# Block 2 of a two-block network: another order of TensorE's work inside a channel block

## The chip, the cores and the metric

The kernel runs on one core of one Trainium2 chip. The metric is the device time of one execution in microseconds; smaller is better. The kernel before has a median of 3219.48 us over 3 runs, from 3214.33 to 3221.94 us. Of the engines this text speaks of PE (TensorE, the matrix engine), DVE (VectorE), ACT (ScalarE), POOL (GpSimd) and SP (the queue that issues the weights' DMAs).

## What is computed

The network takes 1024 tokens of 1024 channels. A first block (two layers of convolution and sparse attention) is followed by a second one, and the change is in the second. There, eight projections of the normalised input are made (`xa`, `ga`, `q`, `f`, `v`, `g`, `m_a`, `m_b`), and two recurrences run over the tokens:

```python
proj = h @ w_in
xa, ga, q, f, v, g, m_a, m_b = jnp.split(proj, SPLIT_POINTS, axis=-1)
xa = causal_depthwise_conv(xa, conv_w, conv_b)
y_a = rg_lru(xa, w_r, b_r, w_i, b_i, lam) * jax.nn.gelu(ga)
...
log_f = jnp.log(jnp.maximum(f_gate, F_MIN))
kf = (1.0 - lb) * jax.nn.sigmoid(-zf)
o = rms_norm(hgrn2_chunkwise(qf, kf, log_f, vf), hg_norm)
y_b = o.reshape(B_, S_, HG_HEADS * HG_DV).astype(h.dtype) * jax.nn.silu(g)
y = jax.nn.sigmoid(m_a) * y_a + jax.nn.sigmoid(m_b) * y_b
return y @ w_out
```

`rg_lru` needs two more products of the convolved `xa`, in blocks of 256 channels: `r` and `i`. `hgrn2_chunkwise` is, for each head of 128 channels, causal linear attention in which the weight of key s for query t is the product of the forget gates between them.

## The kernel before

**Tiling.** The second block works through four channel blocks `b` of 256 channels, that is, two HGRN heads `c` each. A wide product is the sum of three bf16 matmuls (`mm3`, lines 275 to 277: high part by high, low by high, high by low), and its result for 128 channels and all 1024 tokens goes to one of two PSUM tiles of the pool `big`. `gemm_f` makes one such result in two halves of 512 tokens, with a call `between` them. Its eight k-steps are 24 matmuls a half; for `r` and `i` there are only two k-steps, so 6 matmuls a half.

**The order of a channel block on PE** is written out by hand: `xa`, `f`, `q` (two results each), the four tiles `tp` of `v` (token-major, 48 matmuls of 256 columns a tile), and then twelve `units`: r0, i0, r1, i1, ga0, ga1, ma0, ma1, gg0, gg1, mb0, mb1.

**The HGRN steps.** The decayed attention of one head is built by doubling. `hsteps` lists twelve steps for each head: `diag` (line 1004: the products on the diagonal, 8 matmuls of 128 columns in f32), the levels 0 to 6 (line 1052: 8 matmuls of 64 columns in f32), then `tr` (a transposition), `ds`, `o` and `ss`. Between two levels DVE must act: it copies the products under a mask into `PTT` (line 2105), folds the forget gates (line 2112) and scales the half of the queries `QE` and of the keys `KF` that the next level reads (lines 2113 and 2114). After `diag` it copies (line 2083) and multiplies `QE` by the gates (line 2086). So a level on PE waits for DVE, and DVE for the level before. In the kernel before, unit `u` takes the steps `2u` (between the halves of its product) and `2u + 1` (behind it); that puts `diag` and the levels 0 to 6 of head 0 into r0, i0, r1 and i1.

**Other work around it.** ACT evacuates each product in the same order (`evac`, line 1413; the tiles of `v`, line 1443). DVE's queue goes through the convolution, the gates `FG`, the keys `KF` (lines 2066 to 2068), the low part of `xa` (line 2071), and then through the steps in order. POOL splits each weight chunk of 1 MB into its bf16 parts (lines 550 and 557) for a ring of four chunks; it starts a split when PE has finished with the chunk four places earlier (`chunk_used`) and the DMA has landed. The order of chunks is xa, f, q, v, ri, ga, ma, gg, mb, so the end of `v` on PE releases the split of `gg`, and the end of i1 that of `mb`.

Of the kernel before, what the change touches and what calls it, by code (L numbers as in the profile page):

```python
# [23 lines left out]
P = 128  # L24
# [71 lines left out]
def build(nc, ap, events):  # L96

    ctx = ExitStack()
    with ctx:
# [88 lines left out]
        def mark(sem, *what, by=1):  # L188

            counts[sem.name] = counts.get(sem.name, 0) + by  # L190
            assert (sem.name, *what) not in seen, (sem.name, what)
            seen[(sem.name, *what)] = counts[sem.name]
            return by
# [5 lines left out]
        def when(sem, *what):  # L199

            return events[(sem.name, *what)] if events else 1
# [49 lines left out]
        def take(pe, pool, *what):  # L251

            n = turns.get(pool, 0) % len(pools[pool])
            turns[pool] = turns.get(pool, 0) + 1
            out, ids = pools[pool][n]
            if events:
                for before in dict.fromkeys(last_use[i] for i in ids if i in last_use):
                    for sem, value in events[("read", *before)]:
                        pe.wait_ge(sems[sem], value)
            for i in ids:  # L260
                last_use[i] = what
            slot[what] = n
            return out
# [8 lines left out]
        def mm3(pe, out, a, b, start, stop):  # L272

            (ah, al), (bh, bl) = a, b
            pe.matmul(out, ah, bh, start=start, stop=False)  # L275
            pe.matmul(out, ah, bl, start=False, stop=False)  # L276
            return pe.matmul(out, al, bh, start=False, stop=stop)  # L277

        def chunk(l, name, kt):
            n = CHUNK_AT[(l, name)] % RING  # L280
            return [w[:, n, :].rearrange("p (k c) -> p k c", k=kt) for w in (w_hi, w_lo)]
# [124 lines left out]
        units = [("r", 0), ("i", 0), ("r", 1), ("i", 1)] + [(c, n) for c in ("ga", "ma", "gg", "mb") for n in range(2)]  # L406
        FINISH = (10, 11)
        hsteps = [(c, st) for c in range(2) for st in ["diag"] + list(range(7)) + ["tr", "ds", "o", "ss"]]


        ADA_PIECES = [(0, n, kp) for n in range(4) for kp in range(KT // 2)]
# [150 lines left out]
        def _(pe):  # L562
            def gemm_f(l, name, ct, key, rhs=hT, kts=KT, cols=None, pool="big", cw=256, N=T, between=None):

                w = chunk(l, name, CH // cw)
                g = take(pe, pool, *key)
                c0 = ct * P if cols is None else cols[0]
                m = P if cols is None else cols[1] - cols[0]
                for half in range(N // 512):
                    for k in range(kts):  # L570
                        ins = mm3(pe, g[0:m, half * 512:(half + 1) * 512], [x[:, k, c0:c0 + m] for x in w],
                                  [x[:, k, half * 512:(half + 1) * 512] for x in rhs], k == 0, k == kts - 1)
                    if half == 0 and between:
                        between()
                ins.then_inc(s_gemm, mark(s_gemm, *key))

            def chunk_used(l, name, sem):

                seen[("used", CHUNK_AT[(l, name)])] = (sem.name, counts[sem.name])
# [394 lines left out]
            for b in range(4):  # L974
                if b == 0:
                    first_gemm(2, "xa0", [("xa", 0, 0), ("xa", 0, 1)])
                for c in ("xa", "f", "q") if b else ("f", "q"):
# [1 line left out]
                    gemm_f(2, f"{c}{b}", 0, (c, b, 0))  # L979
                    gemm_f(2, f"{c}{b}", 1, (c, b, 1))  # L980
                    chunk_used(2, f"{c}{b}", s_gemm)
                pe.wait_ge(s_w_split, when(s_w_split, CHUNK_AT[(2, f"v{b}")]))
                w = chunk(2, f"v{b}", KT)
                for tp in range(4):
                    g = take(pe, "big", "v", b, tp)
                    for j in range(2):
                        t0 = (2 * tp + j) * P
                        for k in range(KT):
                            ins = mm3(pe, g[:, j * 512:j * 512 + 256], [x[:, k, t0:t0 + P] for x in hT],
                                      [x[:, k, :] for x in w], k == 0, k == KT - 1)  # L990
                    ins.then_inc(s_gemm, mark(s_gemm, "v", b, tp))
                chunk_used(2, f"v{b}", s_gemm)

                def hgrn(c, st):
                    key = (b, c, st)
                    v = VT[:, :, c * P:(c + 1) * P]
# [45 lines left out]
                    else:  # L1042
# [9 lines left out]
                            ins = pe.matmul(g[:, s * 64:(s + 1) * 64].rearrange("p (j h) -> p j h", h=h), KF[c][:, s * P:(s + 1) * P], q, start=True, stop=True)  # L1052
                        ins.then_inc(s_hgrn, mark(s_hgrn, *key))

                for u, (c, n) in enumerate(units):
                    if c in "ri":
                        if u == 0:
                            pe.wait_ge(s_w_split, when(s_w_split, CHUNK_AT[(2, f"ri{b}")]))
                            pe.wait_ge(s_rg_dve, when(s_rg_dve, "xs_lo", b, 1))
                        gemm_f(2, f"ri{b}", None, (c, b, n), rhs=XS, kts=2, cols=((c == "i") * 256 + n * P, (c == "i") * 256 + (n + 1) * P), cw=512,  # L1060
                               between=lambda: hgrn(*hsteps[2 * u]))
                        if u == 3:
                            chunk_used(2, f"ri{b}", s_gemm)
                    else:
                        pe.wait_ge(s_w_split, when(s_w_split, CHUNK_AT[(2, f"{c}{b}")]))
                        gemm_f(2, f"{c}{b}", n, (c, b, n), between=lambda: hgrn(*hsteps[2 * u]))
                        if n == 1:
                            chunk_used(2, f"{c}{b}", s_gemm)
                    hgrn(*hsteps[2 * u + 1])

            def first_two(part, g):
                pe.wait_ge(s_hgrn_dve, when(s_hgrn_dve, "y2_lo", 2, 1))
# [47 lines left out]
        def _(act):  # L1120
# [298 lines left out]
            for b in range(4):  # L1419
# [49 lines left out]
                            freed(s_hgrn_act, "hs", *key, half)  # L1469

                for u, (c, n) in enumerate(units):
                    hgrn(*hsteps[2 * u])
                    if c == "r":
                        act.wait_ge(s_rg_dve, when(s_rg_dve, "xc", b, 1))
                        evac(R_[n], ACT.Sigmoid, "r", b, n, bias=v_("b_r", 2 * b + n))
                    elif c == "i":
                        if b:
                            act.wait_ge(s_rg_dve, when(s_rg_dve, "ya2", b - 1, 1))
                        evac(IT[n], ACT.Sigmoid, "i", b, n, bias=v_("b_i", 2 * b + n))
                        if n == 1:  # L1480
                            act.wait_ge(s_dve_setup, when(s_dve_setup, "sp8"))
                            for m in range(2):
                                act.wait_ge(s_read_act, when(s_read_act, "r", b, m))
                                act.activation(TH[m], R_[m], ACT.Tanh, scale=SP8[:, 2 * b + m:2 * b + m + 1]).then_inc(s_rg_act, mark(s_rg_act, "th", b, m))
                            for m in range(2):
                                act.wait_ge(s_rg_act, when(s_rg_act, "th", b, m))
                                act.activation(R_[m], R_[m], ACT.Exp, scale=NSP8[:, 2 * b + m:2 * b + m + 1]).then_inc(s_rg_act, mark(s_rg_act, "a", b, m))
                    elif c == "ga":
                        if n == 0:
                            for m in range(2):  # L1490
                                act.wait_ge(s_rg_dve, when(s_rg_dve, "one_a2", b, m))
                                act.activation(XC[m], XC[m], ACT.Sqrt).then_inc(s_rg_act, mark(s_rg_act, "mult", b, m))
                        act.wait_ge(s_rg_dve, when(s_rg_dve, "one_a2", b, n))
                        evac(TH[n], ACT.Gelu_apprx_tanh, "ga", b, n)
                    elif c == "ma":
                        act.wait_ge(s_rg_dve, when(s_rg_dve, "ha", b, n))
                        evac(IT[n], ACT.Sigmoid, "ma", b, n)
                    elif c == "gg":
                        act.wait_ge(s_hgrn_dve, when(s_hgrn_dve, "lvl", b, n, 0))
                        evac(FG[n], ACT.Silu, "gg", b, n)  # L1500
                    else:
                        act.wait_ge(s_hgrn, when(s_hgrn, b, n, "tr", 1))
                        evac(KF[n], ACT.Sigmoid, "mb", b, n)
                    hgrn(*hsteps[2 * u + 1])
                    for m in range(2):
                        if u == FINISH[m]:
                            act.wait_ge(s_hgrn_dve, when(s_hgrn_dve, "y2_f", b, m))
                            act.activation(Y2[0][:, 2 * b + m, :], OO, ACT.Copy).then_inc(s_hgrn_act, mark(s_hgrn_act, "y2_hi", b, m))
# [65 lines left out]
        def _(dve):  # L1574
# [473 lines left out]
            for b in range(4):  # L2048
# [71 lines left out]
                def TOT(i):  # L2120

                    at = 1024 - (1024 >> (i - 1))
                    return TB[:, at:at + (1024 >> i)]

                for u, (c, n) in enumerate(units):
                    if (c, n) == ("gg", 0):
                        for m in range(2):
# [5 lines left out]
                        if b < 3:  # L2133

                            dve.wait_ge(s_rg_dve, when(s_rg_dve, "ya2", b, 1))
                            dve.memset(XAP[:, :, 0:3], 0.0).then_inc(s_dve_setup, mark(s_dve_setup, "pad2", b + 1))
                    hgrn(*hsteps[2 * u])
                    hgrn(*hsteps[2 * u + 1])
                    if (c, n) == ("i", 1):
                        for m in range(2):  # L2140
                            dve.wait_ge(s_read_act, when(s_read_act, "i", b, m))
# [250 lines left out]
```

## Time and profile before

| | |
|---|---|
| median of 3 runs | 3219.48 us (3214.33 to 3221.94) |
| profiled execution, span from first to last instruction | 3213.2 us |
| PE busy | 3009.0 us (94%) |
| DVE busy | 1870.8 us (58%) |
| ACT, POOL busy | 1109.3 us (35%), 1033.7 us (32%) |
| granted TensorE clock, mean | 0.966 of 2.4 GHz |
| the four channel blocks of block 2 | about 1512 to 2470 us of the span |

The profile gives one execution. Its span leaves out what lies before the first and behind the last instruction; its own whole time isn't shown, so the median is used beside it, 6.3 us above the span. Starts are in us from the start of the span. In the chain of waits a piece lasts until its successor could go on, and "x16" there is 8 matmuls with their 8 weight loads.

### The profile page before, as it was taken

The numbers are of one execution on the slowest core, as the hardware profiler recorded it, in microseconds if no ns is written. First come the engines' busy times: TensorE is split into PE (matmuls) and PEld (weight loads), VectorE is DVE, ScalarE is ACT, GpSimd is POOL, SyncE is SP. The second block draws the span as 40 slices with busy tenths as digits, with TensorE's granted clock in tenths as the row PEclk, the third lists the DMA queues.
The fourth block names the chain that finished last, engine by engine and source line by source line (L and its number), as shares of the span: only waits on it lengthen the run. The fifth ranks groups of instructions, "written<-read, shape, count | busy, mean of one in ns | idle before, by whom it ended". The sixth has DMA issues, their size and how long they took to land.

```text
span 3213.2 us, 48564 instructions
## 1 busy us (share of the span) xinstructions
PE 3009.0 (94%) x19842; PEld 1864.1 (58%) x19842; DVE 1870.8 (58%) x3077; ACT 1109.3 (35%) x1972; POOL 1033.7 (32%) x1000
## 2 busy tenths in 40 slices
PE   7979987999979978989999999999999989999998
PEld 7439865884439657864555555555565434444443
DVE  2575796773589986644365365365365374545455
ACT  2353545662366635643222222232122221111112
POOL 2301365000512570002512412422322235555552
PEclk9988998999989989999999989999989999999999
DMA  7423232002201330022111101101102101111111
GB/s 243 138 59 106 82 120 86 15 22 99 89 14 43 120 129 28 14 83 77 66 40 40 53 27 40 53 27 40 53 27 92 41 27 53 53 53 53 53 53 73
DMA packets 49165, 207.13 MB, mean 64 GB/s; under 512 B 4488, under 2 KB 9776, under 8 KB 32304
## 3 DMA queue, kind: packets, MB, share of 16 engines
q1 hardware_dynamic: 42288, 195.63, 17.7%
q10 hardware_dynamic: 6656, 8.39, 0.8%
q8 instruction: 158, 2.59, 0.3%
q14 instruction: 63, 0.52, 0.1%
HBM read 187.22 MB, written 16.79 MB: 63 GB/s over the span
## 4 chain that ended last, share of the span: by engine, by line
PE 78%; DVE 16%; ACT 3%; issue 3%; POOL 1%; DMA 0%; SPq 0%; DVEq 0%; ACTq 0%; POOLq 0%
PE big L275 16%; PE big L276 16%; PE big L277 16%; PE banks L275 6%; PE banks L277 5%; PE banks L276 5%; PE banks L1052 4%; DVE arena L1771 2%; PE banks L911 2%; DVE arena L1996 1%; PE big L587 1%; PE banks L587 1%; DVE arena L2160 1%; DVE arena L1976 1%; PE banks L590 1%
## 5 line engine op out<-in xcount | busy, mean ns | idle before, releaser
L557 POOL TENSOR_TENSOR w_lo<-stage,w_hi 128x512 bf16<-128x512 f32 x464 | 594.7, 1315 | 398.2 <-ACT w_hi L1239 397.5
L550 POOL CAST w_hi<-stage 128x512 bf16<-128x512 f32 x376 | 248.6, 704 | 1427.3 <-PE big L277 1232.3
L275 PE MATMUL big<-ht_hi,w_hi 128*128 128x512 bf16 x1184 | 448.7, 379 | 11.7 <-DVE arena L2023 6.5
L277 PE MATMUL big<-ht_hi,w_lo 128*128 128x512 bf16 x1184 | 448.7, 379 | 0.0
L276 PE MATMUL big<-ht_lo,w_hi 128*128 128x512 bf16 x1184 | 448.7, 379 | 0.0
L275 PE MATMUL big<-w_hi,ht_hi 128*128 128x256 bf16 (+1 forms) x1280 | 384.6, 300 | 20.8 <-POOL w_lo L557 9.1
L276 PE MATMUL big<-w_lo,ht_hi 128*128 128x256 bf16 (+1 forms) x1280 | 384.1, 300 | 0.0
L277 PE MATMUL big<-w_hi,ht_lo 128*128 128x256 bf16 (+1 forms) x1280 | 383.4, 300 | 0.0
L1784 DVE TENSOR_SCALAR_CACHE_REDUCE arena<-arena,smalli 128x512 bf16<-128x512 f32 (+5 forms) x268 | 206.7, 827 | 2.4
L275 PEld LDWEIGHTS big<-ht_hi,w_hi 128*128 128x128 bf16 x1184 | 117.6, 99 | 147.9 <-issue 11.4
L277 PEld LDWEIGHTS big<-ht_hi,w_lo 128*128 128x128 bf16 x1184 | 115.8, 98 | 139.7
L275 PE MATMUL banks<-w_hi,arena 128*128 128x128 bf16 (+2 forms) x704 | 178.8, 276 | 17.8 <-ACT arena L1413 9.8
L276 PEld LDWEIGHTS big<-ht_lo,w_hi 128*128 128x128 bf16 x1184 | 115.8, 98 | 132.7 <-issue 3.0
L275 PEld LDWEIGHTS big<-w_hi,ht_hi 128*128 128x128 bf16 x1280 | 150.9, 118 | 62.1 <-issue 10.6
L276 PE MATMUL banks<-w_lo,arena 128*128 128x128 bf16 (+2 forms) x704 | 178.8, 276 | 0.0
L277 PE MATMUL banks<-w_hi,arena 128*128 128x128 bf16 (+2 forms) x704 | 178.8, 276 | 0.0
L2223 DVE TENSOR_TENSOR arena<-arena,banks 128x512 f32<-128x512 f32 x98 | 66.1, 686 | 191.2 <-PE banks L277 191.2
L1315 ACT ACTIVATE arena<-arena,smalli 128x896 bf16<-128x896 f32 x124 | 134.8, 1088 | 114.9 <-DVE smalli L1930 114.9
L277 PEld LDWEIGHTS big<-w_hi,ht_lo 128*128 128x128 bf16 x1280 | 150.4, 117 | 39.1 <-issue 1.6
L276 PEld LDWEIGHTS big<-w_lo,ht_hi 128*128 128x128 bf16 x1280 | 150.3, 117 | 37.7 <-issue 1.1
L2105 DVE COPY_PREDICATED arena<-con,banks 128x512 f32<-128x512 int32 x56 | 58.8, 1050 | 165.0 <-PE banks L1052 164.8
L275 PE MATMUL banks<-arena 128*128 128x128 bf16 (+1 forms) x688 | 145.9, 246 | 6.5 <-DVE arena L2006 5.3
(361 smaller groups left out, 6666.8 us busy)
## 6 DMA issues: line engine op xcount, KB each, us to landing
stage<-in_w SPq DMA_DIRECT2D x130, 1024.0 KB, 4.8
arena<-in_w_ada SPq DMA_DIRECT2D x48, 512.0 KB, 4.3
arena<-in_x SPq DMA_DIRECT2D x16, 512.0 KB, 7.4
xs<-arena SPq DMA_DIRECT2D x16, 512.0 KB, 2.6
arena<-xs SPq DMA_DIRECT2D x16, 512.0 KB, 9.1
gt<-arena ACTq DMA_DIRECT2D x16, 256.0 KB, 2.5
arena<-gt ACTq DMA_DIRECT2D x16, 256.0 KB, 2.7
out_x<-arena SPq DMA_DIRECT2D x8, 512.0 KB, 2.6
```

What stands on the lines that cost most here:

```text
L275: pe.matmul(out, ah, bh, start=start, stop=False)
L276: pe.matmul(out, ah, bl, start=False, stop=False)
L277: return pe.matmul(out, al, bh, start=False, stop=stop)
L550: pool.tensor_copy(w_hi[:, n % RING, c0:c1], stage[:, n % RAW_RING, c0:c1]).then_inc(s_w_hi_split, mark(s_w_hi_split, n, q))
L557: ins = pool.tensor_tensor(w_lo[:, n % RING, c0:c1], stage[:, n % RAW_RING, c0:c1], w_hi[:, n % RING, c0:c1], ALU.subtract)
L587: ins = pe.matmul(g[:, (n * 4 + q) * 8 + k:(n * 4 + q) * 8 + k + 1], ada_buf(i)[:, k % 2, q * P:(q + 1) * P], s_(S_C + k), start=True, sto ...
L911: ins = pe.transpose(g[:, (s - q0) * P:(s - q0 + 1) * P], PB[h % 2][:, s * P:(s + 1) * P], ident)
L1052: ins = pe.matmul(g[:, s * 64:(s + 1) * 64].rearrange("p (j h) -> p j h", h=h), KF[c][:, s * P:(s + 1) * P], q, start=True, stop=True)
L1315: ins = act.activation(is_over[tb], score[tb], ACT.Sign, scale=-1.0, bias=smalli[:, 8 + j:9 + j].bitcast(F32), accum_out=s_(S_CNT + j))
L1771: dve.scalar_tensor_tensor(score[tb], PB[i % 2][:, 0:N], w, score[tb], ALU.mult, ALU.add).then_inc(s_acc, mark(s_acc, l, i))
L1784: ins = dve.tensor_scalar(is_over[tb], score[tb], thr(j), 0.0, op, ALU.add, accum_out=cnt[:, j:j + 1])
L2223: dve.tensor_tensor(out, x, tile("st", "st", j, p), ALU.add).then_inc(s_c_out, mark(s_c_out, j, name))
```

## The change

In the kernel before, PE does the four tiles of `v` back to back, and then r0, i0, r1, i1 with two HGRN steps each. Now each of the four tiles of `v` is followed by one step (`diag`, levels 0, 1, 2 of head 0), and r0, i0, r1, i1 are done whole, with one step behind each (levels 3, 4, 5, 6). From ga0 on the order is as it was. On DVE and on ACT the instructions keep their order, since DVE ran the same steps one after another and ACT has nothing to do in these eight; only the loops are written differently. The definition of `hgrn` on PE moves up ahead of the tiles of `v`, unchanged. `chunk_used` of `v` still names the end of the last tile.

```diff
+        def in_unit(u):
+
+            return hsteps[4 + u:5 + u] if u < 4 else hsteps[2 * u:2 * u + 2]
...
+                for tp in range(4):
+                    g = take(pe, "big", "v", b, tp)
...
+                    ins.then_inc(s_gemm, mark(s_gemm, "v", b, tp))
+                    hgrn(*hsteps[tp])
+                chunk_used(2, f"v{b}", s_gemm)
+
                 for u, (c, n) in enumerate(units):
...
-                        gemm_f(2, f"ri{b}", None, (c, b, n), rhs=XS, kts=2, cols=((c == "i") * 256 + n * P, (c == "i") * 256 + (n + 1) * P), cw=512,
-                               between=lambda: hgrn(*hsteps[2 * u]))
+                        gemm_f(2, f"ri{b}", None, (c, b, n), rhs=XS, kts=2, cols=((c == "i") * 256 + n * P, (c == "i") * 256 + (n + 1) * P), cw=512)
...
-                        gemm_f(2, f"{c}{b}", n, (c, b, n), between=lambda: hgrn(*hsteps[2 * u]))
+                        gemm_f(2, f"{c}{b}", n, (c, b, n), between=lambda: hgrn(*in_unit(u)[0]))
...
-                    hgrn(*hsteps[2 * u + 1])
+                    hgrn(*in_unit(u)[-1])
...
                 for u, (c, n) in enumerate(units):
-                    hgrn(*hsteps[2 * u])
+                    if u >= 4:
+                        hgrn(*in_unit(u)[0])
...
+                for c_st in hsteps[0:4]:
+                    hgrn(*c_st)
                 for u, (c, n) in enumerate(units):
...
-                    hgrn(*hsteps[2 * u])
-                    hgrn(*hsteps[2 * u + 1])
+                    for c_st in in_unit(u):
+                        hgrn(*c_st)
```

## Rows read from the trace of the kernel before

**Rows 1.** The page, part 1: busy time, share of the span, instructions.

```profile
PE 3009.0 (94%) x19842; PEld 1864.1 (58%) x19842; DVE 1870.8 (58%) x3077; ACT 1109.3 (35%) x1972; POOL 1033.7 (32%) x1000
```

**Rows 2.** Waits of PE, 1512 to 2470: total us, times, longest.

```profile
PE banks L1052 <- DVE arena L2114: 20.7, 21, 1.9
PE banks L1052 <- DVE arena L2086: 6.1, 7, 1.4
```

**Rows 3.** Chain of waits, channel block 1, steps of head 0: start, us, what.

```profile
1834.41 0.21 PE big L275
...
1835.71 1.80 PE banks L1004 x16
...
1873.41 1.96 PE banks L1052 x16
1875.38 0.22 PE big L275
```

**Rows 4.** Chain, channel blocks 0, 2 and 3: step diag and level 6.

```profile
1600.78 1.80 PE banks L1004 x16
...
1635.04 2.00 PE banks L1052 x16
...
2073.95 1.80 PE banks L1004 x16
...
2107.33 2.50 PE banks L1052 x16
...
2308.40 1.80 PE banks L1004 x16
...
2347.71 1.81 PE banks L1052 x16
```

**Rows 5.** Chain, channel block 2: levels 2 to 5 of head 0.

```profile
2089.44 2.01 PE banks L1052 x16
...
2094.24 2.01 PE banks L1052 x16
...
2098.69 2.01 PE banks L1052 x16
...
2102.99 2.00 PE banks L1052 x16
```

**Rows 6.** Timeline of ACT, channel block 1: evacuation of q and v tiles.

```profile
1804.47 1.02 ACT L1413 ACTIVATE arena<-big 128x1024 f32<-128x1024 f32 x1
...
1829.21 0.60 ACT L1443 ACTIVATE arena<-big 128x512 f32<-128x512 f32 x1 [4.64 <-PE big L277]
1834.45 0.60 ACT L1443 ACTIVATE arena<-big 128x512 f32<-128x512 f32 x1 [4.64 <-PE big L277]
```

**Rows 7.** Timeline of DVE, channel block 1: keys of head 0, then diag.

```profile
1785.30 0.76 DVE L2067 TENSOR_SCALAR arena<-arena,scol 128x1024 f32<-128x1024 f32 x1
...
1836.64 0.73 DVE L2083 COPY_PREDICATED arena<-con,banks 128x512 f32<-128x512 int32 x1 [33.62 <-PE banks L1004]
```

**Rows 8.** Chain, channel block 1, level 2 of head 1.

```profile
1930.20 1.75 PE banks L1052 x16
...
1935.51 1.53 DVE arena L2114
```

**Rows 9.** Timeline of POOL: splits of two chunks; idle before, releaser.

```profile
1834.55 2.29 POOL L550 CAST w_hi<-stage 128x512 bf16<-128x512 f32 x4 [14.21 <-PE big L277]
...
1930.34 2.29 POOL L550 CAST w_hi<-stage 128x512 bf16<-128x512 f32 x4 [21.36 <-PE big L277]
1932.59 5.45 POOL L557 TENSOR_TENSOR w_lo<-stage,w_hi 128x512 bf16<-128x512 f32 x4
```

**Rows 10.** Stretches: us, busy of PE, PEld, DVE, ACT, POOL; clock; DMA.

```profile
1510.00:1512.00 2.00, 0.00 (x0) 0.00 (x0) 0.99 (x2) 0.91 (x3) 2.00 (x4) 1.00 0.00 0
...
2094.00:2102.00 8.00, 6.59 (x44) 4.65 (x44) 3.62 (x8) 1.11 (x1) 0.00 (x0) 1.00 0.00 0
...
2324.00:2344.00 20.00, 19.76 (x74) 14.10 (x74) 6.98 (x12) 1.11 (x1) 0.00 (x0) 0.50 0.00 0
```

More of the change, by code:

```diff
@@ L981, in _ @@
                     chunk_used(2, f"{c}{b}", s_gemm)
[L982 to L992, printed above, removed]
                 def hgrn(c, st):
@@ L1053, in hgrn @@
                         ins.then_inc(s_hgrn, mark(s_hgrn, *key))
+                pe.wait_ge(s_w_split, when(s_w_split, CHUNK_AT[(2, f"v{b}")]))
+                w = chunk(2, f"v{b}", KT)
+                for tp in range(4):
+                    g = take(pe, "big", "v", b, tp)
+                    for j in range(2):
+                        t0 = (2 * tp + j) * P
+                        for k in range(KT):
+                            ins = mm3(pe, g[:, j * 512:j * 512 + 256], [x[:, k, t0:t0 + P] for x in hT],
+                                      [x[:, k, :] for x in w], k == 0, k == KT - 1)
+                    ins.then_inc(s_gemm, mark(s_gemm, "v", b, tp))
+                    hgrn(*hsteps[tp])
+                chunk_used(2, f"v{b}", s_gemm)
                 for u, (c, n) in enumerate(units):
@@ L1503, in _ @@
                         evac(KF[n], ACT.Sigmoid, "mb", b, n)
-                    hgrn(*hsteps[2 * u + 1])
+                    hgrn(*in_unit(u)[-1])
                     for m in range(2):
@@ L2136, in _ @@
                             dve.memset(XAP[:, :, 0:3], 0.0).then_inc(s_dve_setup, mark(s_dve_setup, "pad2", b + 1))
-                    hgrn(*hsteps[2 * u])
-                    hgrn(*hsteps[2 * u + 1])
+                    for c_st in in_unit(u):
+                        hgrn(*c_st)
                     if (c, n) == ("i", 1):
```

## Prediction

> **What bounds the kernel now.** The page's first part comes first: PE is busy 94% of the span [rows 1], so nearly everything that PE doesn't have to wait for is paid in full, and a change of order can win back only PE's idle time and what a lowered clock costs. The list of PE's waits then says where block 2 idles: over the four channel blocks almost all of its waiting stands before the HGRN levels, for DVE's scaling of the level before (20.7 us in 21 waits) and for its work behind `diag` (6.1 us) [rows 2]. That is 26.8 us of true idleness. The chain of waits over one channel block shows that this isn't the whole loss. In channel block 1 the stretch from `diag` to the first matmul of ga0 takes 1875.38 - 1835.71 = 39.67 us [rows 3]. The same stretch, from the start of `diag` to the end of level 6, is 36.26 us in block 0, 35.88 us in block 2 and 41.12 us in block 3 [rows 4]. With half of r0, which runs before `diag` (1835.71 - 1834.41 = 1.30 us [rows 3]), the four stretches from the last tile of `v` to ga0 are 152.93 + 5.20 = 158.1 us.
>
> The work in one such stretch at the full clock is much less: four products of two halves each, 8 x 1.30 = 10.4 us; `diag`, 1.80 us [rows 3]; and seven levels of 1.75 us when PE doesn't wait in front of them [rows 8]. Together that is 24.5 us, or 98 us for four. So 60 us are lost in the four stretches: 27 to waits, and the rest to the clock. The table of stretches shows the latter: from 2324 to 2344, in channel block 3, PE is busy 19.76 of 20 us at a granted clock of 0.50, the lower level of 1.2 GHz [rows 10]. It got there after a row of short idle gaps between levels.
>
> **Part 1: four steps go behind the tiles of v.** A tile of `v` lasts 5.24 us, from the spacing of its evacuations [rows 6]. The step behind it has two inputs to wait for. The first step needs `QE` and `KF`: `q` of head 0 is evacuated at 1804.47 and the keys are made at 1785.30 [rows 6, 7], while the first tile ends near 1834.45 - 3 x 5.24 = 1818.7, 14 us later. DVE is idle for 33.62 us before `diag` reaches it [rows 7], so all of this stretch is free for it. The later steps need DVE's answer: from the start of level 2 to that of level 3 it takes 4.80 us when nothing disturbs DVE [rows 5], and in the same block the three answers from `diag` to level 2 took 2089.44 - 2073.95 = 15.5 us together, 5.2 us each [rows 4, 5]. PE now fills 1.75 + 5.24 = 7.0 us meanwhile. `diag`, level 0 and level 1 therefore cost PE 1.80 + 2 x 1.75 = 5.3 us and no wait. No product, matmul or DMA is added; the weight chunks are released by the same product ends.
>
> **Part 2: level 2 meets POOL.** Level 2 now starts exactly when the last tile of `v` ends, which is when POOL starts the split of `gg` (1834.55 is 0.1 us behind that end [rows 6, 9]). This meeting stands in the trace already, for head 1: level 2 starts at 1930.20 and POOL's split at 1930.34, and DVE's scaling of the keys takes 1.53 us and ends at 1937.04 [rows 8, 9]. From the start of level 2 that is 6.84 us, and level 3 can start at 6.9, against 4.80 undisturbed [rows 5]. For head 1 it costs PE nothing, as half a wide product (5.2 us) stands between. Here only r0 does, 2.60 us: PE has 1.75 + 2.60 = 4.35 us of work and waits 2.55 us. The bounds for level 2 to level 3 are thus 4.80 and 6.9; I take 6.9, because the row of head 1 has the same start to within 0.1 us. A delayed split costs nothing: `gg` is needed five products later.
>
> The Trainium skill (SBUF — State Buffer, "Who interferes with whom") says that a DVE instruction with two SBUF inputs and a GpSimd instruction that reads SBUF exclude each other for a whole instruction. By that each of DVE's three such operations could wait for one of POOL's, 5.45 / 4 = 1.36 us [rows 9]; the step would then be 4.80 + 3 x 1.36 = 8.9 us, and the sum 8 us worse over four blocks. The row gives 6.9, and I stay with it.
>
> **Part 3: levels 3 to 6 with one whole r or i product each.** Between the starts of two levels PE has 1.75 + 2.60 = 4.35 us of work. DVE's answer takes 4.45 us from level 3 to 4 and 4.30 us from 4 to 5 [rows 5], and from 5 to 6 2107.33 - 2102.99 = 4.34 us [rows 4, 5]. So from level 3 on PE's work and DVE's answer are equal, and the idle time between levels disappears: 4.45 + 4.35 + 4.35 us, and 1.97 us from the start of level 6 to ga0 [rows 3].
>
> **The sum.** A stretch, without the tiles of `v` themselves, becomes 5.3 (`diag`, levels 0 and 1) + 6.9 + 4.45 + 4.35 + 4.35 + 1.97 = 27.3 us. Four are 109.2 us instead of 158.1: 48.9 us less at the full clock.
>
> **The clock** must be taken off. There are now two patterns. With tiles of `v` or the like between the steps, as in the units from ga0 on, the profile of before keeps the full clock. For the part behind level 2 there are rows on both sides. PE idled from 1510 to 1512 entirely, and the clock stayed at 1.00; in channel block 2 it stayed at 1.00 from 2094 to 2102 although PE was idle for 1.4 of 8 us; in block 3 it fell and stayed at 0.50 for over 20 us [rows 10]. The new order has one gap of 2.55 us in a row of small f32 matmuls. Nothing lost (0) and the whole rest of the stretch at half speed (levels 3 to 6 and i0, r1, i1: 4 x 1.75 + 3 x 2.60 = 14.8 us that double) are the bounds for one block. I take 1.75 us a block, an estimate: a fall in about every second block, lasting some 7 us. It is near the lower bound because behind the gap PE is all but continuously busy, which the lowered stretches of before were not when they began. Taken off, 48.9 - 7.0 = 42 us remain: 3219.5 - 42 = **3177 us**. In the profiled execution the span would go from 3213.2 to about 3171.
>
> Behind ga0 I expect nothing to be given back. Level 6 and POOL's split of `mb` keep their places with respect to the end of i1, the evacuations by ACT come in the same order and distance, and PE doesn't wait for weights anywhere in these 950 us (no such line stands beside rows 2). So what is late next is PE itself.
>
> **The rivals.**
> 1. *Level 2 isn't slowed by POOL.* If the split starts a little late, or DVE's operations fall between POOL's, the step takes 4.80 us instead of 6.9. The gap shrinks to 0.45 us, and with it goes the reason for the clock to fall: 158.1 - 4 x 25.2 = 57 us, 3162 us. Against it speaks that level 2 of head 1 shows the slow form. Chance 0.12.
> 2. *The clock falls at the gap in two or three blocks, and stays down until ga0*, as it did in block 3 of before: 48.9 - 2 x 14.8 = 19 us to 48.9 - 3 x 14.8 = 5 us gained, 3200 to 3215 us. For it: levels are small f32 matmuls, and PE was busy 99% of the time from 2324 to 2344 without getting the clock back [rows 10]. Against it: halves of 1.30 us between levels are now whole products, twice as long. Chance 0.12.
> 3. *Slower: the same fall in every block.* Each costs 14.8 us in the place behind level 2, and the gain at the full clock is 12.2 us a block, so the change turns to a loss where a block stays at 1.2 GHz for more than 12.2 / 14.8 = 82% of the rest of its stretch, in all four: 48.9 - 59.2 = -10 us, 3230 us. Against it: channel block 2 of before held the full clock from 2094 to 2102 with a gap before every level [rows 10]. Chance 0.03.
> 4. *It doesn't do what it says:* a step behind `v` waits for something that the stretch did not show, so that the idle time moves forward and the gain is within 6 us: about 3217 us. The 14 us of slack for `diag` and the 33.62 us of idle DVE [rows 7] speak against it. Chance 0.03.
>
> **How the numbers follow.** The forecast (a full or nearly full clock, 0 to 4 us a block lost to it: 3171 to 3187 us) has a chance of 0.70. The range leaves out rivals 3 and 4 and the slower half of rival 2, and takes in rival 1: 3160 to 3200 us. A measurement of this kernel can tell about 0.2%, 6.4 us, from no change. Faster by more than that are the forecast, rival 1 and nearly all of rival 2: 0.93. Within it are rival 4 and a corner of rival 2: 0.04. Slower is rival 3: 0.03.
>
> **What would show it.** In the profile of after: DVE's line 2083 begins within the tiles of `v`, some 20 us ahead of their end, and its idle time before it is about 17 us instead of 33.62. PE's wait list for line 1052 shrinks from 28 waits to about one or two a block, the longest near 2.5 us, in front of level 3. Level 2's DVE operations at line 2113 and 2114 take about 1.5 us each. The distance from the last evacuation of `v` to level 6's end is near 22 us. The clock column behind the gap decides between forecast and rivals 2 and 3. I am wrong if PE waits for weights or for ACT's evacuations in r1 or ga0, if the gap is not there, or if the clock stays at 0.50 there.

## The result and the profile after

The changed kernel takes 3172.85 us (median of 4 runs, 3171.88 to 3174.44) against 3218.86 us for the kernel before beside it: a ratio of 0.9869, with a 95% interval of 0.9854 to 0.9884. The forecast was 3177 us, and 3171 us for the span; the profiled execution spans 3170.1 us. Its busy times answer [rows 1]:

```profile
PE 2964.7 (94%) x19622; PEld 1849.0 (58%) x19842; DVE 1878.9 (59%) x3077; ACT 1109.7 (35%) x1972; POOL 1032.5 (33%) x1000
```

220 of PE's 19842 matmul records are missing in this profile, so its busy time is too small. The repetition described below has them all:

```profile
PE 2980.6 (94%) x19842; PEld 1849.7 (58%) x19842; DVE 1877.0 (59%) x3077; ACT 1108.7 (35%) x1972; POOL 1032.3 (33%) x1000
```

PE is busy 28 us less than in [rows 1] with not one matmul less, while the busy times of DVE, ACT and POOL change by 6.2 us at most. A matmul counts about twice its time at half speed (a step of an r or i product 0.43 us instead of 0.22 in the chain of the changed kernel); that is where busy time can go.

Three views of after show where it came from. First, PE's waits in block 2 (total us, times, longest), beside [rows 2]; line 1044 is now the levels' line, 2119 DVE's scaling of the keys, 2091 its work behind `diag`:

```profile
PE banks L1044 <- DVE arena L2119: 13.5, 8, 2.5
PE banks L1044 <- DVE arena L2091: 0.5, 3, 0.2
```

26.8 us have become 14.0. Of the 8 waits four, of 2.5 us, are the gap in front of level 3 of head 0; the other four, 0.8 to 0.9 us each, and the 0.5 us stand behind ga0, in head 1. Second, the chain through channel block 1 from the end of the last tile of `v` on, beside [rows 3, 8] (start, us, what; 996 is `diag`):

```profile
1828.69 1.75 PE banks L1044 x16
...
1830.56 1.30 DVE arena L2110
1831.87 0.52 DVE arena L2117
...
1832.42 1.51 DVE arena L2118
1833.94 1.57 DVE arena L2119
...
1835.55 2.56 PE banks L1044 x16
...
1841.81 1.73 PE banks L1044 x16
...
1846.13 1.73 PE banks L1044 x16
...
1850.45 1.73 PE banks L1044 x16
```

and, in the same view of a stretch further ahead, where it begins:

```profile
1807.71 1.79 PE banks L996 x16
```

The lines "PE banks L1044" are, from top to bottom, the levels 2, 3, 4, 5 and 6 of head 0. `diag` starts at 1807.71 and ga0 at 1850.45 + 1.73 = 1852.18. Without the three tiles of `v` between them (15.72 us) that is 28.75 us; it was 39.67 + 1.30 = 41.0. From the same two starts (1581.55 and 1624.31, 2033.86 and 2078.26, 2261.68 and 2304.42) the other blocks have 28.8, 30.4 and 28.75 us. Level 3 follows level 2 after 1835.55 - 1828.69 = 6.86 us, level 4 follows level 3 after 6.26 us, then 4.32 and 4.32 us. In the other three blocks level 2 to level 3 takes 6.86 us too, and level 3 to level 4 takes 6.28, 7.92 and 6.26 us. Third, what makes the first of these long is POOL, which starts the split of `gg` at the very end of the tile, as in [rows 9]:

```profile
1828.83 2.28 POOL L554 CAST w_hi<-stage 128x512 bf16<-128x512 f32 x4 [19.48 <-PE big L277]
1831.07 5.44 POOL L561 TENSOR_TENSOR w_lo<-stage,w_hi 128x512 bf16<-128x512 f32 x4
```

What makes the second long is the clock. The table of stretches (columns as in [rows 10]) for a piece of channel blocks 0, 1, 2 and 3 right behind the gap, and the rest of block 1's stretch:

```profile
1612.00:1615.00 3.00, 3.00 (x8) 1.06 (x7) 1.79 (x4) 0.00 (x0) 0.00 (x0) 0.51 0.72 303
1836.00:1841.00 5.00, 5.00 (x24) 3.10 (x23) 2.27 (x4) 0.00 (x0) 0.51 (x1) 0.66 0.59 210
1841.00:1852.00 11.00, 10.95 (x75) 8.00 (x75) 4.17 (x8) 3.68 (x4) 1.41 (x3) 1.00 0.01 1
2062.00:2069.00 7.00, 7.00 (x26) 4.35 (x25) 2.27 (x4) 0.00 (x0) 0.66 (x1) 0.51 0.46 152
2290.00:2295.00 5.00, 5.00 (x24) 3.09 (x24) 2.27 (x4) 0.00 (x0) 0.47 (x1) 0.66 0.62 210
```

The granted clock falls to 0.50 in every block, within some 2 us of the gap's end, for 3 to 4 us in three of them and for more than 6 us in block 2. In the rest of the stretch it is 1.00 with PE busy all the time. The four stretches now take 28.8 + 28.75 + 30.4 + 28.75 = 116.7 us instead of 158.1: 41.4 of the 43.1 us that the spans differ by.

### The profile page after: what moved, and what is told of

It reads as the page before. It is cut to its first block, busy times and chain, and to the rows that moved or that the text cites. A ratio compares the mean times of both kernels' runs of the same rounds, so it can differ in the third digit from the quotient of the medians.

```text
span 3170.1 us, 48344 instructions
## 1 busy us (share of the span) xinstructions
PE 2964.7 (94%) x19622; PEld 1849.0 (58%) x19842; DVE 1878.9 (59%) x3077; ACT 1109.7 (35%) x1972; POOL 1032.5 (33%) x1000
## 4 chain that ended last, share of the span: by engine, by line
PE 78%; DVE 14%; issue 3%; ACT 3%; POOL 1%; DMA 0%; SPq 0%; DVEq 0%; ACTq 0%; POOLq 0%
PE big L276 17%; PE big L277 17%; PE big L275 16%; PE banks L275 6%; PE banks L276 5%; PE banks L277 5%; PE banks L1044 3%; DVE arena L1776 2%; PE banks L915 2%; DVE arena L2001 1%; PE big L591 1%; PE banks L591 1%; DVE arena L2167 1%; DVE arena L1981 1%; PE banks L594 1%
## 5 line engine op out<-in xcount | busy, mean ns | idle before, releaser
L276 PE MATMUL big<-ht_lo,w_hi 128*128 128x512 bf16 x1161 | 440.0, 379 | 4.3 <-DVE ht_lo L1674 1.8
L277 PE MATMUL big<-ht_hi,w_lo 128*128 128x512 bf16 x1163 | 440.8, 379 | 1.2
L275 PE MATMUL big<-ht_hi,w_hi 128*128 128x512 bf16 x1137 | 430.9, 379 | 11.6 <-DVE arena L2028 6.5
L275 PE MATMUL banks<-arena 128*128 128x128 bf16 (+1 forms) x685 | 144.8, 245 | 6.5 <-DVE arena L2011 5.3
```

## The experiments

Each was compared with the kernel before on its own chip. The repetition, the split delayed to level 6, the filled gap and the better order ran on one chip (kernel before: 3219.08 us); the split delayed to level 2, the filled kernel before, the two steps in r0 and i0 and the levels between the halves on another (3214.91 us), where the changed kernel itself wasn't run. A difference of a few us from the changed kernel is therefore safe only for the four of the first chip. "Stretch" is, as in the prediction, the time from `diag` to ga0 without tiles of `v`.

**The changed kernel again**, as the measure for its neighbours.

> The changed kernel once more, beside the three experiments on the same chip. All theories expect about 3173 us, a gap of 2.5 us in front of level 3 in each channel block, and a fall of the granted clock behind it in all or nearly all of the four.

3172.68 us (3172.44 to 3173.5), ratio 0.9861 (0.9844 to 0.9877). The gap and the fall of the clock stand in all four blocks again, so they are there in 8 blocks of 8.

**Does POOL make level 2's answer slow?** The split of `gg` waits for level 6:

```diff
+                if CHUNKS[n][0] == 2 and CHUNKS[n][1].startswith("gg"):
+                    pool.wait_ge(s_hgrn_dve, when(s_hgrn_dve, "lvl", int(CHUNKS[n][1][2:]), 0, 6))
                 by_act = CHUNKS[n][1].startswith("cv")
```

> The changed kernel, but POOL starts the split of the gg weights only when DVE has finished level 6 of head 0. My theory (POOL slows DVE's answer to level 2): level 3 follows level 2 after 4.8 to 4.9 us instead of 6.86, DVE's scaling operations there take 0.6 to 0.7 us instead of 1.6, the gap is 0.5 us and the clock stays up: 16 us less at best. The two splits then run back to back beside DVE's work behind level 6, which may take back up to 2 us a block: 3160 us (3156 to 3168). Rival 'the answer to level 2 is slow for another reason (the place behind the tile of v, PE's reads)': it stays at 6.9 us, 3173 us or more.

3159.87 us (3158.43 to 3161.27), ratio 0.9821 (0.9806 to 0.9836), 12.8 us below the changed kernel. DVE's operations behind level 2 in its timeline, and the levels 2 to 5 in its chain (2112 is the masked copy, 2119 to 2121 the rest; 1046 the levels):

```profile
1827.73 1.30 DVE L2112 COPY_PREDICATED arena<-con,banks 128x512 f32<-128x512 int32 x1 [4.22 <-PE banks L1046]
1828.83 0.32 DVE L2119 TENSOR_TENSOR arena<-arena 128x128 f32<-128x128 f32 x1
1829.07 0.68 DVE L2120 TENSOR_TENSOR arena<-arena 128x512 f32<-128x512 f32 x1
1829.66 0.68 DVE L2121 TENSOR_TENSOR arena<-arena 128x512 f32<-128x512 f32 x1
```

```profile
1825.86 1.75 PE banks L1046 x16
...
1830.40 2.00 PE banks L1046 x16
...
1834.99 1.86 PE banks L1046 x16
...
1839.44 1.73 PE banks L1046 x16
```

The two scalings take 0.68 us each (spans in this view overlap by some 0.1 us) and level 3 follows level 2 after 4.54 us: 0.26 less than the undisturbed 4.80 of [rows 5], because level 2 itself takes 1.75 us when PE did not wait in front of it, and 2.01 when it did. Level 4 follows after 4.59 us and the clock is up:

```profile
1829.00:1850.00 21.00, 20.79 (x128) 13.13 (x127) 10.04 (x21) 10.73 (x10) 1.85 (x4) 1.00 0.00 1
```

So POOL's split is the cause of the slow answer, and the gap goes with it. The two effects are worth 2.3 us and 1.7 us a block (3.3 in block 2), 17.6 us; 12.8 came. A small part is that level 5 follows level 4 after 4.45 us instead of 4.32. The rest is what the expectation allowed for, something given back behind ga0: a stretch is 3.85 us shorter (28.75 to 24.9), but from the `diag` of block 0 to that of block 1 only 2.88 us are gained (223.28 for 226.16). `gg` and `mb` are now split one after the other beside DVE's work behind ga0, where POOL's four subtractions for `gg` take 7.88 us instead of 5.44, and PE waits there for DVE's states (total for the four blocks):

```profile
PE banks L1025 <- DVE arena L2105: 2.3, 4, 0.6
```

So 0.8 to 1.0 us a block are given back, and that line names 0.6 of them. Where the others are wasn't followed up.

**Does the slow answer go where the split goes?** The same edit with level 2 in place of 6 as the last index.

> The changed kernel, but POOL starts the split of gg when DVE has finished level 2 of head 0. My theory: the slow answer moves with the split. Level 3 follows level 2 after 4.8 to 4.9 us, level 4 follows level 3 after 6.3 to 6.6 us, and the gap of some 2 us stands one place further on; the clock falls there. 3172 us (3168 to 3175). Rival 'the slow answer belongs to level 2': its answer stays at 6.9 us.

3175.93 us (3175.83 to 3176.05), ratio 0.9880 (0.9864 to 0.9897). In the chain level 3 follows level 2 after 4.54 us, and now level 3's answer has the two slow scalings, 1.53 and 1.57 us (lines 2120, 2121), so that level 4 follows level 3 after 6.78 us, and runs at half speed itself (3.59 us):

```profile
1831.25 1.75 PE banks L1046 x16
...
1835.79 2.01 PE banks L1046 x16
...
1839.42 1.53 DVE arena L2120
1840.95 1.57 DVE arena L2121
...
1842.57 3.59 PE banks L1046 x16
```

The slowness belongs to the meeting with POOL, not to a level. The time is 1 us over the range given (3168 to 3175). In blocks 1 and 2 level 5 follows level 4 after 7.9 us, in the other two after 6.25: the clock stayed down longer in two blocks instead of one, which costs 1.65 us. That this is the miss isn't shown, since the changed kernel was measured on the other chip.

**Does the idle gap make the clock fall?** PE fills the gap with matmuls whose result nobody reads:

```diff
+                def fill(n, *key):
+                    g = take(pe, "o", "fill", b, *key)
+                    freed(s_gemm, "fill", b, *key)
+                    for i in range(n):
+                        pe.matmul(g[:, :], hT[0][:, 0, 0:P], hT[0][:, 0, 0:512], start=True, stop=True)
...
+                    if u == 0:
+                        fill(11, 0)
                     hgrn(*in_unit(u)[-1])
```

> The changed kernel with 11 idle bf16 matmuls of 512 columns (2.4 us), whose result nobody reads, between r0 and level 3, where PE waits 2.5 us. They add no wait and cannot shorten DVE's answer. My theory (the idle gap makes the clock fall): the clock stays at 1.00 and level 4 follows level 3 after 4.45 us instead of 6.3 to 8.2; 9 us less, 3164 us (3162 to 3167). Rival 'the f32 levels make it fall': clock and time unchanged, 3173 us, or 1 to 2 us more.

3166.29 us (3164.5 to 3166.45), ratio 0.9840 (0.9825 to 0.9854): 6.4 us less by doing more. DVE's answer is as slow as before, level 3 follows level 2 after 6.88 us, but level 4 follows level 3 after 4.60 us (line 1051):

```profile
1829.82 1.75 PE banks L1051 x16
...
1836.70 2.00 PE banks L1051 x16
...
1841.30 1.86 PE banks L1051 x16
...
1845.75 1.73 PE banks L1051 x16
```

```profile
1829.00:1850.00 21.00, 20.82 (x133) 13.48 (x130) 11.40 (x16) 5.22 (x5) 7.71 (x8) 1.00 0.15 51
```

The clock is 1.00 over these 21 us, in which the same f32 levels run, and the other three blocks have the same distances to within 0.02 us. So the idle gap lowers it, and the levels alone don't. The rival is out.

**What was the clock worth in the kernel before?** The same `fill`, of 5 matmuls, in front of each level of head 0 in the kernel before.

> The kernel before with 5 idle bf16 matmuls of 512 columns (1.1 us), whose result nobody reads, in front of each of the levels 0 to 6 of head 0, inside the time in which PE waits. It divides the gain: what the lowered clock cost in the kernel before comes back, what PE's waits cost does not. My theory (the gaps lowered the clock): the clock stays at 1.00 in the r and i stretch, which takes 34.6 us in each block instead of 36.3, 39.7, 35.9 and 41.1; 14 us less than before, 3205 us (3202 to 3210). Rival 'the levels themselves lower the clock': 3219 us or slower.

3201.75 us (3200.8 to 3202.61), ratio 0.9961 (0.9946 to 0.9976), 13.2 us under the kernel before on that chip (3214.91). Its chain in channel block 1, `diag` (line 1013) and level 6 (line 1061):

```profile
1834.41 1.80 PE banks L1013 x16
...
1867.28 2.00 PE banks L1061 x16
```

`diag` to ga0 is 1867.28 + 2.00 - 1834.41 = 34.9 us in place of 39.67 [rows 3], and the other three blocks have the same distances to within 0.1 us. The clock column, 1.00, in this stretch of the filled kernel, and then in the four stretches of the kernel before:

```profile
1834.00:1870.00 36.00, 33.26 (x208) 22.05 (x211) 18.83 (x28) 8.59 (x8) 10.92 (x13) 1.00 0.08 30
```

```profile
1599.50:1637.00 37.50, 30.84 (x177) 20.82 (x176) 18.55 (x27) 8.48 (x9) 10.90 (x13) 0.86 0.09 29
1834.40:1875.40 41.00, 36.56 (x178) 24.96 (x176) 18.14 (x27) 7.11 (x7) 9.59 (x12) 0.71 0.08 26
2072.60:2109.80 37.20, 29.36 (x178) 20.50 (x176) 18.17 (x27) 7.60 (x8) 10.07 (x13) 0.91 0.08 29
2307.10:2349.50 42.40, 38.31 (x178) 26.53 (x176) 18.15 (x27) 6.92 (x7) 9.38 (x11) 0.68 0.08 25
```

By these last rows PE in the kernel before was idle for 158.1 - 135.1 = 23 us in the four stretches, and at clocks of 0.86, 0.71, 0.91 and 0.68 it spent some 68 us at half speed, which is 34 us lost: nearly the whole loss of 60. Yet with the clock at 1.00 only 13 us come back. The two losses hide each other: at half speed PE's own slow work covers DVE's answer, and at full speed that time is idle. The filled kernel gives the size: its four stretches, with the half of r0, take 4 x (34.9 + 1.3) = 144.8 us for the same 98 us of useful work, so at the full clock the order loses some 47 us to waits (filled or not) and slower starts, and not 23. Counted by what a cure brings, the clock alone is worth 13 of the 46 us; the others need work between the levels.

**Does a level need a whole r or i product as cover?** Levels 3 to 6 go two each into r0 and i0, and none into r1 and i1:

```diff
-            return hsteps[4 + u:5 + u] if u < 4 else hsteps[2 * u:2 * u + 2]
+            return hsteps[4 + 2 * u:6 + 2 * u] if u < 2 else [] if u < 4 else hsteps[2 * u:2 * u + 2]
...
+                               between=(lambda: hgrn(*in_unit(u)[0])) if u < 2 else None)
...
```

> Half of the change: diag and levels 0 to 2 stay behind the tiles of v, but levels 3 to 6 go into r0 and i0, two each as in the kernel before (between the halves and behind), and r1 and i1 have none. My theory (a level needs a whole r or i product as cover): level to level is again 4.3 to 4.45 us with 1.75 + 1.3 us of work, so PE idles 1.3 us in front of each; r1 and i1 (5.2 us) come on top: 21 us more than the changed kernel and more lowered clock, 3198 us (3192 to 3206). Rival 'only the steps behind v matter, since PE's work is the same': 3173 us.

3194.74 us (3192.18 to 3203.26), ratio 0.9944 (0.9926 to 0.9961). The four steps behind `v` alone thus give 20.2 us, less than half of the 46, and the levels' even spread the rest. PE's waits are back nearly to [rows 2]:

```profile
PE banks L1044 <- DVE arena L2122: 25.8, 16, 3.8
```

**And is the gap's cover what counts, not the place of a level in its product?** Levels 3 to 6 stand between the halves:

```diff
-                        gemm_f(2, f"ri{b}", None, ..., cw=512)
+                        gemm_f(2, f"ri{b}", None, ..., cw=512,
+                               between=lambda: hgrn(*in_unit(u)[0]))
...
-                    hgrn(*in_unit(u)[-1])
+                    if u >= 4:
+                        hgrn(*in_unit(u)[-1])
```

> The changed kernel with levels 3 to 6 between the halves of r0, i0, r1, i1 instead of behind them. From level to level PE has the same 2.6 us of product; only the cover of the slow answer to level 2 is halved, to 1.3 us. My theory: the gap in front of level 3 grows from 2.5 to 3.8 us, nothing else: 5 us more, 3178 us (3176 to 3184, if the clock stays down longer). Rival 'the gap is hidden by something else': 3173 us.

3181.67 us (3180.13 to 3182.39), ratio 0.9898 (0.9883 to 0.9912). The gap in front of level 3 is 3.8 us at its longest, as expected, with 1.3 us less of cover, and level 3 itself runs at half speed (3.67 us); level 4 follows it after 7.40 us, and level 5 follows level 4 after 4.33 us:

```profile
PE banks L1044 <- DVE arena L2121: 18.7, 8, 3.8
```

```profile
1833.88 1.75 PE banks L1044 x16
...
1840.73 3.67 PE banks L1044 x16
...
1848.13 1.73 PE banks L1044 x16
...
1852.46 1.73 PE banks L1044 x16
```

**A better order.** Every one of the first steps goes one place forward: `diag` behind the last product of `q`, levels 0 to 3 behind the four tiles of `v`, and r0 and i0 both stand between level 3, which now meets POOL's split, and level 4:

```diff
-            return hsteps[4 + u:5 + u] if u < 4 else hsteps[2 * u:2 * u + 2]
+            return hsteps[4 + u:5 + u] if 0 < u < 4 else [] if u == 0 else hsteps[2 * u:2 * u + 2]
...
+                hgrn(*hsteps[0])
                 pe.wait_ge(s_w_split, when(s_w_split, CHUNK_AT[(2, f"v{b}")]))
...
-                    hgrn(*hsteps[tp])
+                    hgrn(*hsteps[1 + tp])
...
```

> The changed kernel with every one of the first steps one place earlier: diag behind the last q product, levels 0 to 3 behind the four tiles of v, no step behind r0, level 4 behind i0, 5 behind r1, 6 behind i1. POOL's split of gg now meets level 3, which has r0 and i0 as cover. My theory (the rest of the loss is the uncovered slow answer and the clock that falls behind it): the gap vanishes (answer of some 6.5 us against 1.75 + 5.2 = 6.95 us of work), the clock stays at 1.00, the stretch from diag to ga0 without the tiles of v falls from 28.8 to about 24.6 us: 17 us less in all, 3156 us (3153 to 3160). Rival 'the clock falls because of the small f32 levels among r and i, gap or no gap': the clock falls still, 3162 to 3167 us. Rival 'what is won ahead is given back behind ga0, by DVE or ACT': 3173 us.

3154.35 us (3152.39 to 3160.81), ratio 0.9807 (0.9792 to 0.9823): 18.3 us under the changed kernel on the same chip. The profiled execution is the one of 3160.81 us, since it reaches the first channel block 6.5 us later than the repetition's does. From there on the gain is all there: a stretch takes 24.45 us for 28.75 (for 30.4 in channel block 2), and nothing is given back behind ga0, as from the `diag` of block 0 to that of block 1 it is 221.84 us for 226.16. PE isn't idle for a moment in the 50 us from before `diag` (1806.41) to the last levels of channel block 1, and the clock is up:

```profile
1800.00:1850.00 50.00, 50.00 (x384) 38.75 (x382) 20.98 (x27) 8.04 (x9) 15.37 (x16) 1.00 0.12 43
```

```profile
1834.36 1.74 PE banks L1044 x16
...
1841.28 1.90 PE banks L1044 x16
```

Level 4 follows level 3 after 6.92 us, all of it PE's own work (1.74 + 5.2). PE's waits for the levels' answers shrink to 0.9 us a block, and these stand in front of level 4 of head 1:

```profile
PE banks L1044 <- DVE arena L2122: 3.4, 4, 0.9
```

## Why the prediction was right

- *What bounds it.* Right: PE's waits for DVE and the lowered clock made the loss, and 60 us was its size. The split into 27 and the rest is right as a count, but not as a price, as the filled kernel before shows. One number was read too widely: of the 26.8 us of waits [rows 2], 3.4 stand in front of level 4 of head 1, as their persistence in the last experiment shows. In block 1 of the kernel before that level starts at 1945.14, 0.9 us after PE's work ahead of it, because DVE has 5.7 us of other work in front of its answer to level 3. The change couldn't touch these waits, and they didn't enter the sum.
- *Part 1* (four steps behind `v`, 5.3 us and no wait): right. Level 0 follows `diag` after 7.03 us, 1.79 + 5.24, so head 0 doesn't wait; the 0.5 us left for `diag`'s answer are head 1's. PE's list has 11 waits, nearly three a block where one or two were expected, 7 of them in head 1. DVE's line for `diag` (2088 now) starts at 1808.64, 20 us before the tiles end, after 16.62 us of idleness where 17 were expected.
- *Part 2* (6.9 us from level 2 to level 3 because of POOL): right to 0.04 us, 6.86, in all four blocks, with DVE's two scalings at 1.51 and 1.57 us. Taking the row of head 1 at its word, and not the undisturbed 4.80, made this term. The delayed split showed that POOL is the cause. The whole-instruction rule of the Trainium skill (SBUF — State Buffer, "Who interferes with whom") agrees with the trace in which operations suffer: only those with two inputs in SBUF are longer in the changed kernel's chain (0.52, 1.51 and 1.57 us) than in the timeline with the delayed split (0.32, 0.68 and 0.68); the masked copy out of PSUM takes 1.30 us in both. The estimate of 8.9 us that I worked out from it, a full wait of 1.36 us each time, was too high by 2 us; by these numbers the two scalings lost 0.8 to 0.9 us each.
- *Part 3* (equal work and answer from level 3 on): right, 4.32 us for 4.35; the end, 1.97 us, was 1.73 since level 6 no longer waits.
- *The clock* is the term that was mis-sized. I had a fall in every second block, 7.0 us in all. It fell in all four. Measured against the 4.45 us that the sum has from level 3 to level 4, it costs 6.26 - 4.45 = 1.8 us in three blocks and about 3.5 in block 2, 8.9 us in all; filling the gap gave back 6.4 us. A fall was more frequent than I had it, and three of the four were half as long; that the two errors nearly cancelled was luck. The end of the stretch, 0.24 us shorter each time than in the sum, took off another 1. So the sum held: four stretches of 116.7 us, where 109.2 + 7.0 = 116.2 were forecast.
- *The rivals.* The fast one (POOL doesn't matter) would have given 3162 us; with the split delayed the kernel makes 3160. The slow ones needed the clock to stay down to ga0, which it didn't do in any block. That whole r and i products bring it back sooner than halves do is argued from the kernel before, and supported by no run of its own.
- *Nothing given back behind ga0*: right for the change, 41.4 of 43.1 us are in the four stretches. It wasn't so for the delayed split.
- *From the span to the median.* The spans differ by 43.1 us, the medians by 46.0. The profiled span of the kernel before lies 6.3 us under its median, that of the changed kernel 2.8 us under its own, so the rows describe one of the quicker executions of the kernel before. What the others lose isn't shown. By the spans the forecast is 0.9 us off (3171 for 3170.1), so most of the 4 us between 3177 and 3172.85 stands in this.

## What to carry to other kernels

When one engine runs a serial chain with another (here PE's level, DVE's answer), list each answer's time and put between two of its steps as much independent work as the answer takes; work that stands in long stretches elsewhere on the engine (the tiles of `v`) is cover that costs nothing. Look at what else the end of a product releases: the answer that meets POOL's weight split needs nearly twice the cover of the others (6.86 - 1.75 = 5.1 us behind the level itself, where 4.54 - 1.75 = 2.8 do otherwise), and moving the steps by one place was worth another 18 us. And count an idle gap on PE twice, once for itself and once for the half speed behind it: here filling 2.4 us with matmuls that nobody reads made the kernel 6.4 us faster.

## What was not expected of the hardware

The regularity of the fall: a gap of 2.5 us in front of an f32 level, behind a short bf16 product, was followed by the lower clock in 8 of 8 blocks, each time within some 2 us, while PE's full idleness from 1510 to 1512 between wide bf16 products had left the clock at 1.00 [rows 10]. What makes the difference, the kind of work around the gap or the moment at which it comes, stays open; no run varied it. In the better order the same levels, with no gap, kept 1.00.
